# Strassen's product for 16 of the 22 up pairs of each FFN in a float32 encoder layer

## The reference: what is computed

```python
def _rms(x, g):
    y = xf * lax.rsqrt(jnp.mean(xf * xf, axis=-1, keepdims=True) + EPS)
    return (y * g.astype(jnp.float32)).astype(x.dtype)

def _swiglu(h, w_up, w_down):
    gate, up = jnp.split(h @ w_up, 2, axis=-1)
    return (jax.nn.silu(gate) * up) @ w_down
...
        x = x + 0.5 * _swiglu(_rms(x, g_ffn1[l]), w_up1[l], w_down1[l])
        h = _rms(x, g_mix[l])
        z = h @ w_in[l]
...
        x = x + (gate_a * y_a + gate_b * y_b) @ w_out[l]
        x = x + 0.5 * _swiglu(_rms(x, g_ffn2[l]), w_up2[l], w_down2[l])
    return _rms(x, g_final)
```

## Time and profile before

| what | value |
|---|---|
| time before, median of 3 runs | 1036.88 us (1035.63 to 1037.46) |
| the profiled execution's own time | 1037.65 us |
| its span, first to last instruction | 1035.9 us |
| PE busy | 1022.5 us (99%) |
| chain that ended last, share of PE | 94% |
| DVE busy | 496.9 us (48%) |
| ACT busy | 394.4 us (38%) |
| POOL busy | 51.4 us (5%) |
| HBM traffic | 97 GB/s over the span |

### The profile page before, as it was taken

The page is one execution under the profiler, slowest core; times in us unless marked ns, Lnnn a source line. Parts: engine busy times, 40 slices in busy tenths (PEclk is TensorE's granted clock), DMA queues, the critical chain, the costliest instruction groups (busy, mean ns, idle before and its releaser), DMA issues.

```text
span 1035.9 us, 13119 instructions
## 1 busy us (share of the span) xinstructions
PE 1022.5 (99%) x4720; PEld 851.6 (82%) x4720; DVE 496.9 (48%) x724; ACT 394.4 (38%) x555; POOL 51.4 (5%) x49
## 2 busy tenths in 40 slices
PE   8999999999999999999999999999999999999997
PEld 7788888888888888978888888888888888888887
DVE  5564444443334346667765555445444454423332
ACT  5333332332223235346664333425445434233322
POOL 3100000000011010000000002200000000000001
PEclk9999999999999999999999999999999999999999
DMA  6399973222332463212213343323333332233222
GB/s 210 104 128 133 104 134 101 87 85 69 99 96 84 121 176 95 89 41 62 62 42 92 97 136 102 102 60 113 109 87 98 101 100 78 63 99 97 84 69 82
DMA packets 191150, 100.76 MB, mean 97 GB/s; under 512 B 12224, under 2 KB 189456, under 8 KB 190992
## 3 DMA queue, kind: packets, MB, share of 16 engines
q1 hardware_dynamic: 189280, 95.49, 31.4%
q0 software_dynamic: 640, 2.10, 5.9%
q10 hardware_dynamic: 1200, 2.76, 0.8%
HBM read 96.15 MB, written 4.19 MB: 97 GB/s over the span
## 4 chain that ended last, share of the span: by engine, by line
PE 94%; DVE 1%; ACT 1%; POOL 1%; issue 1%; DMA 1%; SPq 0%; POOLq 0%; ACTq 0%
PE bank L1058 30%; PE bank L1059 30%; PE bank L1070 29%; POOL ssum L1013 1%; PE bank L1280 1%; DMA x_rows<-in_x_dram 1%; PE bank L1063 1%; PE bank L1036 1%; PE bank L1040 1%; PE bank L1035 1%; PE bank L1297 0%; PE bank L1107 0%; ACT w_hi L471 0%; PE bank L1294 0%; PE bank L1295 0%
## 5 line engine op out<-in xcount | busy, mean ns | idle before, releaser
L718 DVE TENSOR_TENSOR w_lo<-raw,w_hi 128x1024 fp32r<-128x1024 f32 (+3 forms) x202 | 227.6, 1127 | 336.9 <-ACT w_hi L471 335.2
L1058 PE MATMUL bank<-h_hi,w_hi 128*128 128x512 f32 x912 | 357.5, 392 | 1.6 <-DVE ga_t L854 1.6
L1059 PE MATMUL bank<-h_lo,w_hi 128*128 128x512 f32 x912 | 356.0, 390 | 0.0
L471 ACT ACTIVATE w_hi<-raw 128x1024 fp32r<-128x1024 f32 (+3 forms) x202 | 189.2, 937 | 233.8 <-PE bank L1070 229.7
L1070 PE MATMUL bank<-h_hi,w_lo 128*128 128x512 f32 x888 | 224.2, 390 | 0.0
L1058 PEld LDWEIGHTS bank<-h_hi,w_hi 128*128 128x128 f32 x912 | 172.0, 189 | 38.1 <-DVE ga_t L854 1.8
L1059 PEld LDWEIGHTS bank<-h_lo,w_hi 128*128 128x128 f32 x912 | 171.9, 188 | 35.4 <-issue 0.2
L1070 PEld LDWEIGHTS bank<-h_hi,w_lo 128*128 128x128 f32 x888 | 166.7, 188 | 35.6 <-issue 1.0
L1058 PE MATMUL bank<-a_hi,w_hi 128*128 128x512 f32 (+1 forms) x374 | 140.1, 379 | 0.0
L1059 PE MATMUL bank<-a_lo,w_hi 128*128 128x512 f32 (+1 forms) x374 | 139.3, 377 | 0.0
L1070 PE MATMUL bank<-a_hi,w_lo 128*128 128x512 f32 (+1 forms) x374 | 91.1, 377 | 0.0
(11 more groups left out here) (190 smaller groups left out, 834.2 us busy)
## 6 DMA issues: line engine op xcount, KB each, us to landing
raw<-in_w_up_dram SPq DMA_DIRECT2D x88, 512.0 KB, 3.8
raw<-in_w_down_dram SPq DMA_DIRECT2D x32, 384.0 KB, 3.0
raw<-in_w_in_dram SPq DMA_DIRECT2D x22, 512.0 KB, 3.7
raw<-in_w_down_dram SPq DMA_DIRECT2D x32, 320.0 KB, 2.8
raw<-in_w_out_dram SPq DMA_DIRECT2D x8, 512.0 KB, 3.4
x_rows<-in_x_dram SPq DMA_DIRECT2D x4, 512.0 KB, 6.9
bias_rows<-bias_row POOLq DMA_DIRECT2D x8, 256.0 KB, 11.2
raw<-in_w_in_dram SPq DMA_DIRECT2D x8, 256.0 KB, 3.4
```

The source lines that it names most:

```text
L471: return nc.scalar.activation(dst, src, ACT.Copy, scale=scale)
L718: vec.tensor_tensor(w_lo[:, s, 0:nk, :], raw[:, s, 0:nk, :], w_hi[:, s, 0:nk, :].bitcast(F32), ALU.subtract).then_inc(w_lo_ready, 1)
L1058: nc.tensor.matmul(out_ap, w_hi[:, s, k, :], xh, start=first and i == 0, stop=False)
L1059: mm = nc.tensor.matmul(out_ap, w_hi[:, s, k, :], xl, start=False, stop=False)
```

## The change

In each FFN the first `DIRECT` = 6 pairs stay as they were. The other `PAIRS` = 16 are computed by Strassen's method in the form with seven products: the weights of a pair are a 2 x 2 matrix of blocks (gate or up by lower or upper half of the input features, 128 x 4 x 128 each), the activations are one too (lower or upper half of the features by first or second half of the positions, 4 x 256 columns each). Seven sums of activation blocks (`t_sum`, split into `t_hi` and `t_lo`) are made once for each FFN, from activations that are already normalized (L1036). For each pair, DVE and POOL form the sums of weight blocks, and PE does 7 products of 4 blocks by 3 passes by 256 columns (84 matmuls of 256) where it did 48 of 512. The products stand in four **groups** of weights: G0 and G1 and G2 with two blocks of 4 x 128 each, G3 with one. G3's product for pair q is done in the frame of pair q + 1.

The weights of a pair now land as a whole in one of two buffers (`raw_b` for even q, `raw` for odd q), in four transfers of 256 KB:

```diff
+            def window_loads(r, q, it=0):
+
+                if q:
+                    sp.wait_ge(w_lo_ready, G_WIN[r] + SLOTS * q - SLOTS + 1 + 2 * SLOTS * it)
+                for a, group, at_, row in ((0, G0, 0, 0), (0, G1, 0, HK), (1, G1, HK, HK), (1, G3, HK, 0)):
...
+                    sp.dma_start(pair_raw[q % 2][:, pair_slot(r, group), at_:at_ + HK, :],
+                                 w_up[r][:, row:row + HK, cols]).then_inc(pair_landed[q % 2], 16)
```

For q of 2 and more that wait is for the rest of G3 of pair q - 2. DVE's frame (its work during pair q), and POOL's:

```diff
+            def sums(r, q, it=0):
...
+                dve.wait_ge(pair_landed[q % 2], 64 * (PAIRS // 2 * r + q // 2 + 1) + 64 * it)
+                vec.tensor_tensor(s13[:, HK:DK, :], a11, a21, ALU.subtract).then_inc(s13_ready, 1)
+                vec.tensor_tensor(s13[:, 0:HK, :], a21, a22, ALU.add).then_inc(s13_ready, 1)
...
+            def pair_frame(r, q, it=0):
+
+                if q:
+                    c2(r, q - 1, it)
+                sums(r, q + 1, it)
+                if q:
+                    group_lo(r, q, G2, it)
+                u2(r, q, it)
+                if q:
+                    c12(r, q - 1, it)
+                group_lo(r, q + 1, G0, it)
+                group_lo(r, q, G3, it)
+                if q:
+                    swiglu(r, q - 1, it)
+                group_lo(r, q + 1, G1, it)
...
+                    for q in range(PAIRS):
...
+                        pool.wait_ge(s13_ready, 2 * (PAIRS * r + q) + 1)
+                        nc.gpsimd.tensor_tensor(s2, a22, s3, ALU.subtract).then_inc(s2_ready, 1)
+                        pool.wait_ge(s2_ready, PAIRS * r + q + 1)
+                        nc.gpsimd.tensor_tensor(blk[:, pair_slot(r, G3), 0:HK, :], a12, s2,
+                                                ALU.subtract).then_inc(s4_ready, 1)
```

`c2`, `u2` and `c12` add products out of the banks (256, 512, 256 and 256 columns), `swiglu` is gate by up. ACT rounds the groups (`group_hi`), G0 after `s2_ready` and G3 after `s4_ready`:

```diff
+            def pair_frame(r, q, it=0):
+
+                group_hi(r, q, G2, it) if q else None
+                first_product(r, q, it)
+                group_hi(r, q + 1, G0, it)
+                if q:
+                    silu_c12(r, q - 1, it)
+                group_hi(r, q, G3, it)
+                silu_c11(r, q, it)
+                group_hi(r, q + 1, G1, it)
```

PE's frame is the seven products in the order G0, G0, G3 of pair q - 1, G1, G1, G2, G2:

```diff
+            def pair_frame(r, q, it=0):
...
+                product(r, q, it, G0, 0, T_B11, x_ap).then_inc(p1_done, 1)
...
+                product(r, q, it, G0, HK, T_2, y_ap).then_inc(w_used, 1)
+                if q:
+                    last_product(r, q - 1, it)
+                pe.wait_ge(p1_ready, PAIRS * r + q + 1 + 2 * it)
+                product(r, q, it, G1, 0, T_B21, x_ap, first=False).then_inc(c11_done, 1)
...
+                product(r, q, it, G1, HK, T_4, z[:, 0:HALF]).then_inc(w_used, 1)
+                product(r, q, it, G2, 0, T_1, z[:, HALF:SEQ])
+                pe.wait_ge(u2_ready, PAIRS * r + q + 1 + 2 * it)
+                product(r, q, it, G2, HK, T_3, y_ap, first=False).then_inc(w_used, 1)
```

More of the change, by code:

```diff
@@ L76 @@
 HALF = SEQ // 2
+T_B11, T_2, T_B21, T_4, T_1, T_3, T_B22, T_B12 = range(8)
+T_ORDER = [T_B11, T_1, T_2, T_B21, T_4, T_3, T_B22]
+HK = DK // 2
+G0, G1, G2, G3 = range(4)
+W_X, W_Y = [4, 5], [6, 7]
+CONV = [0, 1, 2, 3, 4, 5, 7, 8, 6, 9, 10]
 NPOS = SEQ // 2 + 2
@@ L179, in granule_tiles, with landed, window_count @@
     return DK
+def landed(g):
+    return 16 * (g // SLOTS + 1 - PAIRS * sum(g >= down for down in G_DOWN))
+def window_count(q, group):
+    if group == G3:
+        return SLOTS * (q + 1)
+    if group == G0:
+        return SLOTS * q - 1 if q else 0
+    return SLOTS * q + group
 def turn_index(u, b):
@@ L539, in ffn_up, with bias_pieces @@
-                    copy(tile(a_hi, 2 * it + j), up_t[j][:, :]).then_inc(a_hi_ready, 1)
+                    if d < DIRECT - 2:
+                        split_hi(g + 1 + SLOTS, it, n)
+                    elif d == DIRECT - 2:
+                        group_hi(r, 0, G1)
+                    if r == 0 and d >= 2:
+                        bias_pieces(2 * (d - 2), 2)
+                if d == DIRECT - 1:
+                    t_rounded(r, T_3)
+                    t_rounded(r, T_B22)
+            def bias_pieces(head, count):
+                act.wait_ge(row_ready, 1)
+                for i in range(head, head + count):
+                    act.dma_start(bias_rows[i:i + 1, :, :], bias_row[i:i + 1, :].unsqueeze(1).broadcast_to([1, P, SEQ])
+                                  ).then_inc(bias_stored, 16)
@@ L566, in _ @@
             for r in range(2):
-                with act.Fori(0, FK // 2 - 1) as it:
+                for it in range(DIRECT // 2):
                     ffn_up(r, it)
-                ffn_up(r, FK // 2 - 1)
+                pair_frame(r, 0)
+                with act.Fori(0, PAIRS // 2 - 1) as it:
+                    pair_frame(r, 1, it)
+                    pair_frame(r, 2, it)
+                last_pair(r)
                 if r == 0:
@@ new lines, in last_pair @@
+            def last_pair(r):
+                q, g = PAIRS - 1, G_DOWN[r]
+                c2(r, q - 1)
+                group_lo(r, q, G2)
+                u2(r, q)
+                a_rest(r, 0)
+                c12(r, q - 1)
+                split_lo(g)
+                group_lo(r, q, G3)
+                swiglu(r, q - 1)
+                a_rest(r, 1)
+                a_rest(r, 2)
+                split_lo(g + 1)
+                c2(r, q)
+                a_rest(r, 3)
+                split_lo(g + 2)
+                a_rest(r, 4)
+                a_rest(r, 5)
+                c12(r, q)
+                a_rest(r, 6)
+                swiglu(r, q)
+                split_lo(g + 3)
+                for i in (7, 8, 9, 10):
+                    a_rest(r, i)
@@ L1145, in ffn_up @@
                         pe.wait_ge(x_ready, DK)
[L1146 removed]
+                    granule(g, banks[o % BANKS][:, :], hf_parts, it=it, n=n, by_tile=first and j == 0,
                             x_ready_at=h_ready(nrm) if first and j == 0 else None,
```

354 lines of the change are left out of this document (298 added, 56 removed).

## The result

| | median | runs | range |
|---|---|---|---|
| before | 1036.43 us | 4 | 1035.63 to 1037.46 |
| after | 1137.95 us | 4 | 1136.1 to 1140.95 |

The ratio is 1.098, 95% interval 1.096 to 1.099: slower, as forecast, but by 101.5 us instead of 40, and outside the range. The span of the profiled execution is 1136.8 us.

What follows compares the result with a forecast made beforehand. PE's stream bounded the kernel; afterwards a 12.17 us ring of load, DVE and POOL work would. (18.5 + 1.5) x 2 = 40.0 us on 1037.65 gave 1077.7, stated as 1077; 8-in-10 range 1038 to 1105.

Steps and rivals of the forecast that it cites:

- the ring: Strassen frames: load, DVE's sums and rests, next load follow serially; one turn 12.17 us, 15 turns an FFN, +18.5 us each.
- the other edits: Changes outside the Strassen frames: activation sums free, hidden-activation splits +1.5 us per FFN, transfers on ACT's queue zero.
- the activation sums: Direct pairs 1 to 5: DVE's and POOL's added sums cost nothing under DVE's idle time; without cover up to 23 us per FFN.
- the lock: POOL and DVE operations with SBUF operands wait for each other, so their times in the ring add up to 6.88 us.
- PE's new stream: Strassen frames: 84 matmuls of 256 columns at 0.120 us, 10.08 us a pair against 10.88; gains 25.6 us without waits.
- My upper bound of 5.8: A pair's four weight loads: 3.8 us plus 2.0 for a second 512 KB at 260 GB/s; 5.1 was taken.
- the second place of the earlier trace: DVE and POOL operations overlapping at 631.95 us: together 2.37 us against 2.52, 0.15 less for each POOL operation.
- The down start: Start of the down phase: PE waits for DVE's ninth split of the hidden activation, done at 11.2 against 9.7; +1.5 us each.
- 1 (short transfer): A pair's four loads overlap nearly wholly, landing in 3.8 to 4.3 us: 1038 to 1053 us; chance 0.12.
- 2 (POOL beside DVE): POOL's weight subtractions run beside DVE, -8.8 us per FFN before +1.5: 1022, or 1014; chance 0.17 together with the fourth rival.
- 3 (the clock falls): PE's gaps in the frames lower its clock; often, or with all bounds at their far end, 1100 to 1120; above 1100: 0.09.
- 4 (0.130 us a matmul): 256-column matmuls take 0.130 us instead of 0.120, frames 10.9; changes only the second rival, to about 1040; jointly 0.17.

Runs made afterwards that it cites:

- experiment 1: Changed kernel with the eight `bias_rows` transfers moved from FFN 1's direct pairs to its down tiles, one per tile: 1102.91 us.
- experiment 7: experiment 1's kernel with DVE taking G3's rest before the next pair's sums, G0's rest behind them, ACT rounding in that order: 1042.92 us.
- experiment 8: experiment 7's kernel with the two weight-block subtractions `s2` and `s4` moved from POOL to DVE: 1027.49 us.
- experiment 11: Changed kernel with bias transfers in the down phase, G3's rest before the sums, weight subtractions and activation sums on DVE, first product's copy earlier: 1022.27 us.
- experiments 1 to 3: Changed kernel, `bias_rows` transfers all in down tiles, 1102.91 us; four in direct pairs singly, 1103.93; two per pair with 16 of 128 rows, rest in down tiles, 1100.64.
- Experiment 4: `bias_rows` transfers on POOL's queue, one at a time, in Strassen frames 0 to 7 of FFN 1: 1147.76 us, 44.9 above experiment 1.
- experiment 5: experiment 1's kernel with two of each pair's four weight loads left out from the third Strassen pair on, output no longer right: 1036.70 us.

## Why the prediction was wrong

The 101.5 us lost, and more, are accounted for by steps that each ran:

| step | us | what it takes away |
|---|---|---|
| after, 1137.95 to experiment 1, 1102.91 | 35.0 | transfers of `bias_rows` beside loads and ACT |
| to experiment 7, 1042.92 | 60.0 | the ring |
| to experiment 8, 1027.49 | 15.4 | POOL beside DVE in the frames |
| to experiment 11, 1022.27 | 5.2 | POOL beside DVE ahead of them, the late copy |

**The step that failed** is the last of the other edits: "The transfers on ACT's queue are a few issues beside idle time. Zero." I counted their issues, not what they move. They cost 35 us, and experiments 1 to 3 show that it is their time on the DMA engines, two per pair: with the same issues and an eighth of the rows the 35 us are gone. The view of the kernel before that has their price (11.2 us each, loads of 9.1 beside them) is one that I hadn't used for them. Experiment 4 adds that in the frames, where the loads have lost their lead, even one at a time costs 44.9 us.

**Other edits, the activation sums.** "So they cost nothing" fell too. POOL's four sums are not spread over direct pairs 1 to 5: they stand back to back in 12.0 us (774.71 to 786.73 in FFN 2), and hold DVE up by 3.7 of the 5.9 us shown above; the subtractions of pair 0 behind them do the rest. I used the lock in the ring and forgot it here. DVE's 5.84 us of idle time a pair are real, but part of it is a wait for ACT between a rounding and its rest; that late work can't use this part is an argument, not a measurement. The price after, in FFN 2: 4.1 + 0.9 us of PE's waits, and 16 matmuls in 3.5 us instead of 1.9 while the clock was half.

**The sum without the bias transfers.** The forecast of 1077 is 25.9 us short of 1102.9. In FFN 2 after, from PE's first product (797.06) to its first down granule (1001.13, behind a wait of 1.06) pass 203.0 us, where the sum had 8.64 + 182.6 = 191.2. 15 turns of 12.59 are 188.9, so 6.3 us are the turns'. What is left, 14.1 instead of 8.64, gives 5.5 us to frame 0 and to the last frame, which has no sums. Twice that and twice 0.5 at the down start are 24.6 us.

**PE's new stream**: right. 10.08 us a frame was measured in experiments 8 and 11 to the hundredth.

**The ring of waits**: right in mechanism, and shown by order alone (7). Its size was 12.59 us instead of 12.17, and that it was so near is partly luck, since two errors have opposite signs (0.87 too little and 0.52 too much, by the frame shown):
- transfer and issue 6.16 instead of 5.29 with its gaps. The four loads don't run at the 349 to 377 GB/s of the earlier trace rows; each costs 1.08 us more (experiment 5), 243 GB/s. My upper bound of 5.8, from the rate inside one load, was the better reading, and still 0.2 short.
- DVE and POOL 6.36 instead of 6.88. From the sums to the operation behind G2's rest pass 157.72 - 154.27 = 3.45 us (the sum: 1.20 + 1.14 + 1.29 = 3.63), from there to the end of G3's rest 2.91 (the sum: 0.13 + 1.29 + 1.14 + 0.69 = 3.25). POOL's operations begin while DVE's still run (155.04, 156.79), so a strict sum is a little too much, as the second place of the earlier trace rows had shown: 0.15 us for each was measured there, some 0.26 here. `u2` and `c12` took 0.41 beside `s4`, as alone, so the 0.7 us of the upper bound weren't needed. That `s4` "ends before ACT's 1.06 us of rounding is over" doesn't follow from its own terms (0.13 + 1.29), and it didn't (158.94 against 157.88); the sum had counted `s4` in full, so nothing hangs on it.
- What PE waits for: `c2`, as said, 0.65 us in the frame shown; but the longer wait, 1.4, is for G2's rest and not for G0's. The forecast's time doesn't depend on it.

**The down start**: predicted +1.5, measured 1.1 + 0.9 = 2.0 us of PE's waits per FFN. The size is right but for 0.5, the reason is not: PE waits 1.1 us ahead of the first down granule for ACT's rounding of weights, which the sum didn't have, and 0.9 us ahead of the third for ACT's rounding of the activations, not for DVE's ninth split.

**The rivals.** 1 (short transfer): out, 5.98. 2 (POOL beside DVE): out, by the rests of 2.32. 3 (the clock falls): not in the frames, whose gaps of 1.4 and 0.7 us left it at 1.00 (150 to 174 us), but in or after the stops of 4 us and more (0.50 at 100 to 110 and at 806 to 808 us). 4 (0.130 us a matmul): out. Rival 2's -8.8 us per FFN leaves out that the first frame is shorter too; with it, it is -9.5, which changes nothing.

## What to carry to other kernels

A transfer is priced by its time on the DMA engines, not by its issue: before moving one, read how long the same one took to land and what landed beside it. Where a load is issued by the last reader of its buffer, put that reader ahead of any wait for the next landing; the order on one engine was worth 60 us here, more than all arithmetic that the algorithm saved (25.6). Cover on an engine isn't the sum of its idle time: ask what that idle time waits for, and whether the added work of another engine locks it.

## What was not expected of the hardware

- A transfer that writes one partition's row 128 times (256 KB) took 11.1 to 11.2 us (median) with no other of its kind in flight, and held the DMA engines at 0.87 to 0.90 share with 27 to 28 GB/s (experiment 1, 311 to 317 us). Several together took 25.4 us each (median), and the issuing engine then stood up to 13.1 us at its own issues.
- Four loads of 256 KB behind each other on one queue: 5.98 us from the first issue to their use, two of them 3.83.
- PE, idle for about 4 us between dense products, was then granted 0.50 of its clock (1.2 of 2.4 GHz) in the windows of 806 to 808 us; idle for 1.4 us it kept 1.00.
